# Other order of the head of a fused two-block layer kernel: filler transposes, loads and split work before the first projections

## The reference, cut to what matters

```python
mod = jax.nn.silu(c) @ w_ada[l] + b_ada[l]            # (1, 6144)
sh1, sc1, g1, sh2, sc2, g2 = jnp.split(mod, 6, axis=-1)
u = modulate(rmsnorm(h, norm_mix_g[l]), sh1, sc1)     # (256, 1024)
z = u @ w_in[l]
rq, rk, rv, rg, dq, dkv, iq, ik, iw = _split_cols(z, IN_SPLITS)
```

## Time and profile before

| what | us |
|---|---|
| median of three runs | 733.33 (732.9 to 733.6) |
| the profiled execution, its own time | 732.7 |
| its span, first to last instruction | 731.4 |
| TensorE busy | 709.5 (97%) |
| VectorE busy | 513.8 (70%) |
| ScalarE busy | 379.6 (52%) |
| GpSimd busy | 54.4 (7%) |
| bytes read from HBM | 162.33 MB |

### The profile page before, as it was taken

One profiled execution on the slowest core, in us unless ns is written; L12 is line 12 of the kernel. 1 busy time (PEld: TensorE's weight loads), 2 busy tenths in 40 slices (PEclk: granted clock), 3 DMA queues, 4 the chain that ended last, 5 costly groups with the idle time before them and its releaser, 6 DMA issues.

```text
span 731.4 us, 9904 instructions
## 1 busy us (share of the span) xinstructions
PE 709.5 (97%) x3754; PEld 570.3 (78%) x3754; DVE 513.8 (70%) x759; ACT 379.6 (52%) x549; POOL 54.4 (7%) x68
## 2 busy tenths in 40 slices
PE   4999999999999999999999999999999999999997
PEld 2887666767888877888877777779888887888886
DVE  1456897536687774785668988887998665656854
ACT  3334435555436354474457877648533547644442
POOL 0002110240020000000000000011003400000000
PEclk9999999999999999999999999999999999999999
DMA  9999688588346931856589999945434574545541
GB/s 288 348 281 384 239 304 302 201 322 313 119 164 227 333 107 58 264 174 196 177 259 349 362 364 360 356 159 169 148 116 143 165 218 141 169 141 187 167 138 58
DMA packets 104894, 164.07 MB, mean 224 GB/s; under 512 B 10896, under 2 KB 53613, under 8 KB 104718
## 3 DMA queue, kind: packets, MB, share of 16 engines
q1 hardware_dynamic: 102942, 155.54, 64.4%
q0 software_dynamic: 1904, 7.90, 3.1%
HBM read 162.33 MB, written 1.08 MB: 223 GB/s over the span
## 4 chain that ended last, share of the span: by engine, by line
PE 83%; DVE 9%; ACT 3%; DMA 3%; issue 1%; SPq 0%; POOL 0%; ACTq 0%; DVEq 0%; POOLq 0%
PE p L568 23%; PE p L570 22%; PE p L569 22%; DVE s_rawr L1870 3%; PE p L637 2%; PE p L626 2%; PE p L1254 2%; DMA s_raw<-in_w_gate_dram 2%; PE p L683 1%; DMA s_GS<-in_w_ada_dram 1%; PE p L1083 1%; ACT s_hi L1415 1%; ACT s_L L1465 1%; PE p L707 1%; PE p L695 1%
## 5 line engine op out<-in xcount | busy, mean ns | idle before, releaser
L1870 DVE TENSOR_TENSOR s_rawr<-s_raw,s_hi 128x1024 fp32r<-128x1024 f32 x240 | 286.8, 1224 | 50.5 <-ACT s_hi L1415 50.0
L1415 ACT ACTIVATE s_hi<-s_raw 128x1024 fp32r<-128x1024 f32 x240 | 244.9, 1054 | 109.7 <-PE p L570 47.1
L568 PE MATMUL p<-s_hi,s_Ah 128*128 128x512 f32 (+1 forms) x464 | 187.4, 404 | 1.1 <-DVE s_rawr L1870 0.7
L570 PE MATMUL p<-s_hi,s_Al 128*128 128x512 f32 (+1 forms) x464 | 179.6, 387 | 0.0
L569 PE MATMUL p<-s_rawr,s_Ah 128*128 128x512 f32 (+1 forms) x464 | 179.4, 387 | 0.0
L568 PEld LDWEIGHTS p<-s_hi,s_Ah 128*128 128x128 f32 x464 | 87.2, 188 | 30.5 <-issue 10.2
L570 PEld LDWEIGHTS p<-s_hi,s_Al 128*128 128x128 f32 x464 | 87.1, 188 | 18.5
L569 PEld LDWEIGHTS p<-s_rawr,s_Ah 128*128 128x128 f32 x464 | 87.4, 188 | 16.0 <-issue 0.5
L568 PE MATMUL p<-s_hi,s_Bh 128*128 128x512 f32 x192 | 76.3, 397 | 0.5 <-DVE s_BI L2441 0.3
L570 PE MATMUL p<-s_hi,s_Bl 128*128 128x512 f32 x192 | 74.9, 390 | 0.0
L569 PE MATMUL p<-s_rawr,s_Bh 128*128 128x512 f32 x192 | 74.8, 390 | 0.0
(11 more groups left out here) (380 smaller groups left out, 854.3 us busy)
## 6 DMA issues: line engine op xcount, KB each, us to landing
s_raw<-in_w_in_dram SPq DMA_DIRECT2D x80, 512.0 KB, 4.8
s_raw<-in_w_exp_gate_dram SPq DMA_DIRECT2D x64, 256.0 KB, 4.0
s_raw<-in_w_exp_up_dram SPq DMA_DIRECT2D x64, 256.0 KB, 5.0
s_raw<-in_w_exp_down_dram SPq DMA_DIRECT2D x32, 512.0 KB, 5.5
s_GS<-in_w_ada_dram SPq DMA_DIRECT2D x12, 1024.0 KB, 7.4
s_raw<-in_w_gate_dram SPq DMA_DIRECT2D x16, 512.0 KB, 9.6
s_GS<-in_w_ada_dram SPq DMA_DIRECT2D x8, 512.0 KB, 8.9
s_raw<-in_w_ret_out_dram SPq DMA_DIRECT2D x8, 512.0 KB, 3.6
```

Of the source, the lines that this page charges most:

```text
L568: pe.matmul(o, xh, wh, start=start, stop=False)
L570: return pe.matmul(o, xl, wh, start=False, stop=stop)
L1415: act.activation(T.hi[:, i % NHL, :], T.raw[:, i % NRAW, :], ACT.Copy).then_inc(*S.hi(i))
L1870: dve.tensor_tensor(T.lo[:, i % NRAW, :], T.raw[:, i % NRAW, :], T.hi[:, i % NHL, :].bitcast(F32), ALU.subtract).then_inc(*S.lo_dve(i))
```

## The change

1. TensorE: 44 idle transposes directly behind the transpose of c. The two halves of product 0 are issued apart, with `u_cols(0)` between them. Behind the rows 4 idle transposes in place of 8, then `head_sum(0)`, `u_cols(2)`, and 28 in place of 24.
2. SyncE: piece 0, ada 2 and 3, pieces 1 to 3, ada 4 and 5, pieces 4 to 6, ada 6 and 7, pieces 7 to 9.
3. SyncE: the four router loads go from behind the constants to the place ahead of ada 18 and 19.
4. ScalarE: the high half of piece 0, then that of the columns 0, then pieces 1 to 3; piece 4 alone ahead of the columns 4; pieces 5 to 8 behind them and ahead of the columns 6; piece 9 behind those.
5. VectorE: the low halves stand at other places among the copies, sums and columns.

```diff
     for r0, c in ((39, 0), (55, 3072)):
         sp.dma_start(T.VR[r0:r0 + 16, :], ...)
+    pieces(1)
+    ada(2), ada(3)
     pieces(3)
-    ada(2), ada(3)
-    pieces(2)
     ada(4), ada(5)
     pieces(3)
     ada(6), ada(7)
-    pieces(2)
+    pieces(3)
...
-    sp.dma_start(T.WR[:, :, 0:4], ...)
-    sp.dma_start(T.WR[:, :, 4:20], ...)
-    sp.dma_start(T.RB[:, 0:4], ...)
-    sp.dma_start(T.RB[:, 4:20], ...)
     pieces(AT["rk", 0] - done[0])
     for i, then in ((8, ("rv0", 2)), ..., (16, ("ga0", 3)), (18, ("ro1", 3))):
+        if i == 18:
+            (the same four loads)
         ada(i), ada(i + 1)
         pieces(AT[then] - done[0])
```

```diff
     pe.transpose(PT[0][:, 0:8], T.VRC[:, :], ident[0:8, 0:8]).then_inc(*S.pe_head("c"))
     t_free[0] = S.act_head.at("cs")
+
+    keep_busy(44)
     q.wait_ge(*S.act_head.at("cs"))
-    head_ada(0)
+    ada(0, PZ[1], ((0,),))
+    u_cols(0)
+    ada(0, PZ[1], ((1,),))
     q.wait_ge(*S.rows_in.at(0))
     pe.transpose(PT[1][:, 0:71], T.VR[0:71, :], ident[0:71, 0:71]).then_inc(*S.pe_head("rows"))
...
-    keep_busy(8)
-    u_cols(0)
+    keep_busy(4)
     head_sum(0)
     u_cols(2)
-    keep_busy(24)
+    keep_busy(28)
```

```diff
# ScalarE
+    his(1)
+    high_of("uF", T.uF, 0, T.Ah, "u")
     his(3)
-    high_of("uF", T.uF, 0, T.Ah, "u")
-    his(2)
     full_cols("uF", T.uF, 2, T.Ah, "u", scale, shift, S.dve_head.at("m", 1))
-    his_to(AT["iq", 2] + 1)
+    his_to(AT["dq", 2])
     high_of("uF", T.uF, 4, T.Ah, "u")
+    his_to(AT["dq", 3])
+    full_cols("uF", T.uF, 6, T.Ah, "u", scale, shift, S.dve_head.at("m", 3))
     his_to(AT["rq", 0])
-    full_cols("uF", T.uF, 6, T.Ah, "u", scale, shift, S.dve_head.at("m", 3))
# VectorE
     ada_copy(0)
-    lows_to(1)
     q.wait_ge(*S.pe_head.at("rows"))
     dve.tensor_copy(T.VC[:, 8:79], T.PT[1][:, 0:71]).then_inc(*S.dve_head("rows"))
     ada_end(0)
     modulation(0)
     affine("uF", "u", T.uF, 0, scale, shift, S.dve_head.at("m", 0))
+    lows_to(1)
     low_of("u", T.uF, 0, T.Ah, T.Al)
-    lows_to(AT["dq", 1])
     ada_copy(1)
-    lows_to(AT["iq", 1])
+    lows_to(AT["iq", 0])
     ada_end(1)
     modulation(1)
+    lows_to(AT["iq", 1])
     low_of("u", T.uF, 2, T.Ah, T.Al)
+    ada_copy(2)
     lows_to(AT["dq", 2])
-    ada_copy(2)
-    lows_to(AT["kv", 1])
     ada_end(2)
     modulation(2)
     affine("uF", "u", T.uF, 4, scale, shift, S.dve_head.at("m", 2))
+    lows_to(AT["kv", 1])
     low_of("u", T.uF, 4, T.Ah, T.Al)
+    lows_to(AT["iq", 2])
+    ada_copy(3)
     lows_to(AT["iq", 3])
-    ada_copy(3)
     ada_end(3)
     modulation(3)
```

More of the change, by code:

```diff
@@ L433, in sp_program @@
         sp.dma_start(T.WKV[:, 64 * j:64 * j + 64], I["w_dsa_kv_up"][:, 64 * (j // 2):64 * (j // 2) + 64]).then_inc(*S.wkv_in(0))
[L434 to L437, removed]
     pieces(AT["rk", 0] - done[0])
     for i, then in ((8, ("rv0", 2)), (10, ("rv1", 2)), (12, ("rg0", 2)), (14, ("ga0", 0)), (16, ("ga0", 3)), (18, ("ro1", 3))):
+        if i == 18:
+            sp.dma_start(T.WR[:, :, 0:4], I["w_group_router"].rearrange("(k p) n -> p k n", p=128)).then_inc(*S.route_in(0))
+            sp.dma_start(T.WR[:, :, 4:20], I["w_expert_router"].rearrange("(k p) n -> p k n", p=128)).then_inc(*S.route_in(0))
+            sp.dma_start(T.RB[:, 0:4], I["b_group_router"].broadcast_to([128, 4])).then_inc(*S.route_in(0))
+            sp.dma_start(T.RB[:, 4:20], I["b_expert_router"].broadcast_to([128, 16])).then_inc(*S.route_in(0))
         ada(i), ada(i + 1)
@@ L728, in pe_program, with u_cols, keep_busy @@
     A, B, C = (T.Ah, T.Al), (T.Bh, T.Bl), (T.Ch, T.Cl)
+    def u_cols(k0):
+        q.wait_ge(*S.dve_head.at("xr", 1))
+        turn(lambda tt, k: T.XR[:, tt, 128 * k:128 * k + 128], ("u", k0), (S.act_cols if k0 % 4 else S.dve_cols).at("uF", k0))
+    def keep_busy(n):
+        for _ in range(n):
+            pe.transpose(PZ[0][:, 0:128], ident, ident)
     q.wait_ge(*S.c_in.at(0))
@@ L739, in pe_program @@
     t_free[1] = S.dve_head.at("rows")
-    def u_cols(k0):
-        q.wait_ge(*S.dve_head.at("xr", 1))
-        turn(lambda tt, k: T.XR[:, tt, 128 * k:128 * k + 128], ("u", k0), (S.act_cols if k0 % 4 else S.dve_cols).at("uF", k0))
     def u(h):
@@ L760, in kv_piece @@
             r.then_inc(*S.piece("kv", h, 1))
-    def keep_busy(n):
-        for _ in range(n):
-            pe.transpose(PZ[0][:, 0:128], ident, ident)
-    keep_busy(8)
-    u_cols(0)
+    keep_busy(4)
     head_sum(0)
     u_cols(2)
-    keep_busy(24)
+    keep_busy(28)
     for n in range(3):
```

## The result

| | before | after |
|---|---|---|
| median | 733.6 us (732.9 to 733.88, 5 runs) | 737.58 us (736.82 to 738.63, 5 runs) |
| profiled execution, its own time | 732.7 us | 736.82 us |
| its span | 731.4 us | 735.5 us |
| TensorE busy | 709.5 us | 715.0 us |

The ratio is 1.0058, 95% interval 1.0046 to 1.0070: slower by 4.0 us where 3.3 were forecast. TensorE is busy for 5.5 us more: the 44 idle transposes take 7.5 us, a stretch at half speed costs 1.5 us more, and some of the head's work has become faster.

A forecast was written before the change was run, and what follows sets the result against it. TensorE, busy for 97% of the span, was taken as the bound. Terms -2.4 + 2.0 + 1.65 + 2.05 = +3.3 us took the profiled 732.7 to 736.0, as a median 736.6; range 735.4 to 739.0.

The forecast's parts named there:

- The earlier start: Head of TensorE: idle transposes moved forward raise the clock, so dq0 starts at 19.35, 2.4 us earlier.
- kv0: Projection after product 1: waits 2.0 us for the low half of piece 1, now behind ada_copy(1) on VectorE.
- Part 2: The step on halves behind the copy: kv0 waits 2.0 us because of VectorE's order, not the transfer.
- iq0: Projection behind head_sum(1): waits 1.65 us for the low half of piece 2, now behind ada_end(1) and modulation(1).
- dq2: Projection after iq1: waits 2.05 us for the columns 4, as VectorE makes the low half of piece 5 first.
- The sum of the order: Whole kernel: earlier start of 2.4 us against waits of 2.0, 1.65 and 2.05 gives +3.3 us.
- Nothing from the router's loads: SyncE: the loads' 6.1 us fit into 17.2 us of waiting ahead of ada 18; no cost or gain.
- the term of the clock: TensorE's clock in the new gaps: no fall assumed, since a 1.1 us wait had kept its level.
- the rival of one fall: Clock falls in one of the new gaps, about 4.4 us at half speed, 2.2 us lost: 738.8; chance 0.09.
- Part 5: Pieces 4 and 7, chunk loads and router's loads cost nothing; each chunk load lands no later than before.

The follow-up runs named there:

- x10_loads: A third order of halves and loads, with the change's load order and ScalarE's piece 1 behind the columns 0; 731.8 us, ratio 0.9988 to the kernel before.
- x3_fill: The changed kernel with idle transposes in its three gaps: 17 before kv0, 12 before iq0, 18 before dq2; 735.92 us, ratio 1.0037 to the kernel before.
- x1_p2: The changed kernel with VectorE making the low half of piece 2 ahead of ada_end(1); 736.42 us, ratio 1.0039 to the kernel before.
- x2_p5: The changed kernel with piece 5 split ahead of the columns 4 on ScalarE and ahead of ada_end(2) on VectorE; 734.52 us, ratio 1.0025 to before.
- x8_both: The changed kernel with the edits of x1_p2 and x2_p5 together; 732.06 us, ratio 0.9997 to the kernel before.
- x5_router: The kernel before with the four router loads moved alone; 733.2 us, ratio 1.0005 to the kernel before.
- the second: The changed kernel, unaltered, measured again beside the experiments in six runs; 738.92 us, ratio 1.0070 to the kernel before.
- x4_pe: The kernel before with TensorE's part of the change alone (44, 4 and 28 idle transposes, u_cols(0) inside product 0); 733.7 us, ratio 1.0009.
- x9_rows_first: x4_pe with the low half of piece 0 moved behind affine(0) on VectorE; 732.31 us, ratio 0.9991 to the kernel before.

## Why the prediction was right

The time lies in the range, and each of the waits that were to carry it is in the profile at its place and of its size. The cause given for the first of them, before kv0, was half of the truth, and the clock was left out.

- *The earlier start*, -2.4: measured -2.44, dq0 at 19.29 for the 19.35 forecast. Transposes alone raised the clock. The earlier trace rows were weak evidence for that, as the products ran on TensorE at 12.81, just ahead of the transposes; the kernel after shows it plainly. The 44 end at 10.9 instead of 10.5, as the rise came at 8.6 and not at 7.9. The sentence of the Trainium skill ("TensorE: Matmul & The Clock Gate", section on transposes) that they don't count does not hold here: nothing but transposes ran between 3.34 and 10.86, and behind the 25th they became fast (7.5 us for the 44, where 44 at 0.213 would be 9.4).
- *kv0*, +2.0: the wait is 1.95. But Part 2 says of the transfer that it is "not the reason either", and that is wrong. In x10_loads the low half stands ahead of the copy, and kv0 still waits 1.78 us for it. Part 2's own numbers say so: a high half ready at 24.1 and 1.22 us for the low one make 25.3, and kv0 was free to start at 24.24. That the size came out all the same was luck: the copy ends some 0.5 us behind the high half (about 24.9 against 24.4), and only the later of the two counts.
- *iq0*, +1.65: the view says 1.35, but it counts from the end of the last transpose, at 28.77; from the place at which iq0 could have started, 27.73 + 0.79 = 28.52, to 30.12 it is 1.6.
- *dq2*, +2.05: the view says 2.03.
- The sum of the order, +3.3: x3_fill, in which the clock does not fall, is 3.1 slower. x1_p2 and x2_p5 each take one term away, x8_both takes both, and each takes its own waits and no other. The term of kv0 was never taken away by moving VectorE's half alone, other than in x10_loads, where it stayed.
- *Nothing from the router's loads*: x5_router.

**What was mis-sized** is the term of the clock. I took it as zero, "as the nearest row has none", and gave the rival of one fall 0.09. In truth the granted clock was 0.998 or less in every one of the eleven runs of the changed kernel, and the term measured 1.5 us in the profiled execution and up to some 4 in others (740.06 less the 735.92 of x3_fill). Without the clock the order's 3.3 falls short of the first measurement (4.0) by 0.7 us and of the second (738.92 against 732.81, 6.1) by 2.8. The first median lies at the upper bound of the order's terms (737.6); the second lies in the range only because the range took in the one fall that I held unlikely. The nearest row, a wait of 1.1 us, was too short to speak for gaps of 2 us; in hindsight three such gaps within 20 us should have had a chance of over one half, and the forecast would have been 738. The rival's own price, 2.2 us for a fall, was too high by 0.7: the stretch lasted 3.4 us and not 4.4, and the matmuls in it stood 0.213 us apart instead of 0.119, less than twice, for sixteen of them 1.5 us.

Part 5 was right in its result. Its "each lands no later than before" holds for the modulation loads and not for piece 1, which landed at 23.3 instead of 17.2, as Part 2 had it; the price of that is in the wait before kv0.

Open is why a given execution falls behind one gap and not behind another. Open is also why the wait for ada 19 goes away: it is in the four profiles without the 44 transposes (0.3 to 0.4 us) and in none of the ten with them, whether their later work is early or late. That was seen, not tried.

## What to carry to other kernels

Where one engine is busy all the time, a start that is 2 us earlier is worth only what the written orders of the engines feeding it let through: walk each in-order queue and ask what the next wanted product stands behind; here three waits for low halves cost 5.6 us against 2.4 won, and another order of the same halves and loads turned the same start into a gain of 2.7. Ask it of the load too: behind one late half the next cause may already stand, and mending the first alone wins little. Put work that needs only a load ahead of work that waits for the busy engine, unless its load is late, and order the loads by the same list. And count a gap in TensorE's work twice: by its length, and by the half speed that may follow.

## What was not expected of the hardware

- Of thirteen gaps of 1.8 to 2.0 us in TensorE's work, in the nine profiles that have such gaps, eight were followed by 3.4 or 6.8 us at half its clock. Two gaps of 1.35 us were not. Over eleven runs of one kernel this made times from 736.19 to 740.06. Filled with idle transposes (x3_fill), the runs lie within 0.5 us.
- The first rise comes at different times for the same instructions: 19.0 in the profiled execution of the kernel before, 18.0 in x5_router with the same work on TensorE; and between 6.5 and 8.8 in the ten profiles with 44 transposes from 3.3 on.
- A wait hidden by a slower start comes to light when the start is earlier: the bank of the rows (1.93 us, x4_pe), the high half of piece 2 (1.8 us, x9_rows_first).
